# FFN down stage: M7, two slots of M3, M4, the rest of M3, M2; token chunks 0 and 1 updated, normed and turned within it

## What is computed

```
def rmsnorm(x, w):
    y = xf * lax.rsqrt(jnp.mean(xf * xf, axis=-1, keepdims=True) + RMS_EPS)
    return (y * w.astype(jnp.float32)).astype(x.dtype)

def swiglu(h, w_gate, w_up, w_down):
    return (jax.nn.silu(h @ w_gate) * (h @ w_up)) @ w_down

Layer i:  x += 1/2 * post(SwiGLU_1(pre(x)))
          x += post(Mixer_i(pre(x)))   Mixer_even = [GLA heads | Mamba-2 SSD heads], Mixer_odd = MLA
          x += 1/2 * post(SwiGLU_2(pre(x)))
```

## Time and profile before

| | |
|---|---|
| median of 3 runs | 2123.82 us (2123.49 to 2124.54) |
| profiled execution | 2123.88 us |
| its span | 2121.9 us |
| TensorE busy | 2086.2 us, 98% |
| VectorE busy | 1257.0 us, 59% |
| ScalarE busy | 865.7 us, 41% |
| mean granted TensorE clock | 0.993 |
| HBM traffic | 174 GB/s over the span |

### The profile page before, as it was taken

The page is one execution under the profiler, slowest core; times in us unless marked ns, Lnnn a source line. Parts: engine busy times, 40 slices in busy tenths (PEclk is TensorE's granted clock), DMA queues, the critical chain, the costliest instruction groups (busy, mean ns, idle before and its releaser), DMA issues.

```text
span 2121.9 us, 26132 instructions
## 1 busy us (share of the span) xinstructions
PE 2086.2 (98%) x10362; PEld 1750.5 (82%) x10362; DVE 1257.0 (59%) x1819; ACT 865.7 (41%) x1255; POOL 88.7 (4%) x79
## 2 busy tenths in 40 slices
PE   9999999999999999999999999999999999999998
PEld 8888877888888888988887788888787779888877
DVE  6444567476666644645457755445775646445576
ACT  5222355444545543422235532224545444222354
POOL 0000001000000000000000100000014100000000
PEclk9999999999999999999999999999999999999999
DMA  7566684232111213565677375757733124666694
GB/s 267 204 232 211 216 310 154 85 93 60 60 60 60 70 55 134 199 237 199 226 251 264 126 259 191 238 204 259 254 104 125 55 70 143 215 220 226 199 319 142
DMA packets 144412, 371.28 MB, mean 175 GB/s; under 512 B 10354, under 2 KB 10994, under 8 KB 144291
## 3 DMA queue, kind: packets, MB, share of 16 engines
q1 hardware_dynamic: 83440, 229.14, 34.0%
q10 hardware_dynamic: 60850, 140.47, 17.4%
HBM read 297.22 MB, written 71.30 MB: 174 GB/s over the span
## 4 chain that ended last, share of the span: by engine, by line
PE 92%; DVE 4%; issue 2%; ACT 1%; POOL 1%; DMA 0%; ACTq 0%; POOLq 0%; DVEq 0%
PE ps L1137 18%; PE ps L1139 18%; PE ps L1138 18%; PE ps L1145 9%; PE ps L1147 9%; PE ps L1146 9%; PE ps L1452 1%; DVE w_lo L1786 1%; PE ps L1671 1%; PE ps L1700 1%; PE ps L1164 1%; PE ps L1520 1%; DVE normed L1792 1%; PE ps L1675 1%; PE ps L1376 1%
## 5 line engine op out<-in xcount | busy, mean ns | idle before, releaser
L1137 PE MATMUL ps<-h_hi,w_hi 128*128 128x512 f32 (+1 forms) x1832 | 683.3, 373 | 12.9 <-DVE h_lo L1786 12.6
L1139 PE MATMUL ps<-h_hi,w_lo 128*128 128x512 f32 (+1 forms) x1832 | 677.2, 370 | 0.0
L1138 PE MATMUL ps<-h_lo,w_hi 128*128 128x512 f32 (+1 forms) x1832 | 677.1, 370 | 0.0
L577 ACT ACTIVATE w_hi<-raw 128x1024 fp32r<-128x1024 f32 x432 | 454.2, 1057 | 527.3 <-PE ps L1139 338.6
L1786 DVE TENSOR_TENSOR w_lo<-raw,w_hi 128x1024 fp32r<-128x1024 f32 x417 | 502.6, 1221 | 152.2 <-ACT w_hi L577 151.1
L1137 PEld LDWEIGHTS ps<-h_hi,w_hi 128*128 128x128 f32 x1832 | 348.4, 190 | 72.2 <-DVE h_lo L1786 13.9
L1139 PEld LDWEIGHTS ps<-h_hi,w_lo 128*128 128x128 f32 x1832 | 348.3, 190 | 57.7
L1138 PEld LDWEIGHTS ps<-h_lo,w_hi 128*128 128x128 f32 x1832 | 348.6, 190 | 55.9 <-issue 0.2
L1786 DVE TENSOR_TENSOR extra<-a_rows,ps 128x512 f32<-128x512 f32 x88 | 60.5, 688 | 404.0 <-PE ps L1139 380.9
L1145 PE MATMUL ps<-w_hi,a_split 128*128 128x512 f32 x616 | 241.6, 392 | 9.3 <-DVE update L1786 9.3
L1146 PE MATMUL ps<-w_lo,a_split 128*128 128x512 f32 x616 | 240.6, 391 | 0.0
(11 more groups left out here) (237 smaller groups left out, 2233.9 us busy)
## 6 DMA issues: line engine op xcount, KB each, us to landing
raw<-in_w_gate_up SPq DMA_DIRECT2D x176, 512.0 KB, 4.6
a_rows<-in_w_down ACTq DMA_DIRECT2D x44, 1024.0 KB, 9.7
sums<-a_rows ACTq DMA_DIRECT2D x44, 1024.0 KB, 7.8
raw<-sums SPq DMA_DIRECT2D x80, 512.0 KB, 5.2
raw<-in_w_down SPq DMA_DIRECT2D x60, 512.0 KB, 5.3
spilled<-extra ACTq DMA_DIRECT2D x44, 512.0 KB, 4.8
normed<-spilled ACTq DMA_DIRECT2D x44, 512.0 KB, 5.9
raw<-in_w_vg SPq DMA_DIRECT2D x16, 512.0 KB, 3.5
```

Source lines behind the costliest of these rows:

```text
L577: return nc.scalar.activation(to, source, ACT.Copy, scale=scale)
L1137: nc.tensor.matmul(to, w_h, hi, start=first, stop=False)
L1138: nc.tensor.matmul(to, w_h, lo, start=False, stop=False)
L1139: return nc.tensor.matmul(to, w_l, hi, start=False, stop=last)
```

## The change

The order becomes M7 (six slots), M3 (two), M4 (six), M3 (four), M2 (six). Refinements and reloads get new places. Chunks 0 and 1 go through squares, update, norm and turn inside the stage. The sums c21 and c11 are written to rows of their own (`late_sum`, in `extra`) instead of over `update`, and `scale_late` writes their scaled form to `update`. The diff, cut:

```diff
-    for m in range(GROUPS - 2):
-        order += [("M7", m), ("M3", m)]
-    order += [(name, m) for name in ("M7", "M3") for m in (GROUPS - 2, GROUPS - 1)]
-    return order + [("M4", m) for m in range(GROUPS)] + [("M2", m) for m in range(GROUPS)]
+    order += [("M7", m) for m in range(GROUPS)] + [("M3", m) for m in range(2)] + [("M4", m) for m in range(GROUPS)]
+    return order + [("M3", m) for m in range(2, GROUPS)] + [("M2", m) for m in range(GROUPS)]
...
-REFINED_AFTER = [min(2 * j + 4, 23) for j in range(PAIRS)]
+REFINED_AFTER = [3 + (9 * j + 2) // 5 for j in range(PAIRS)]
 JOB_PAIRS = (6, 2)
-RELOAD_AFTER = [min(2 * j, 19) for j in range(PAIRS)]
+RELOAD_AFTER = [max(0, REFINED_AFTER[j] - 5) for j in range(PAIRS)]
...
+        late_sum = [extra[:, (2 + c) % 4, :] for c in range(NC)]
...
+                if b - 1 in FFN_OF:
+                    root_f(b, 0)
+                    root_f(b, 1)
+                    if b < N_SUB:
+                        root_x(b, 0)
+                        root_x(b, 1)
+                for c in range(2 if b - 1 in FFN_OF else 0, NC):
...
                     act.wait_ge(c21_done if c < 2 else c11_done, 2 * FFN_OF[b - 1] + c % 2 + 1)
-                    mean_square(chunk(update, c, 0), stat(SSF1, b, c))
+                    mean_square(late_sum[c], stat(SSF1, b, c))
...
+                if b - 1 in FFN_OF:
+                    square0(b, 2)
+                    square0(b, 3)
+                    if b < N_SUB:
+                        split_high(first)
+                        high_of_h(b, 0)
+                        split_high(first + 1)
+                        high_of_h(b, 1)
+                    square1(b, 2)
+                    if b < N_SUB:
+                        split_high(first + 2)
+                        square_x(b, 2)
+                        split_high(first + 3)
+                    square1(b, 3)
+                    if b < N_SUB:
+                        if b == ODD:
+                            odd_inputs()
+                        high_of_h(b, 2)
+                        square_x(b, 3)
+                        high_of_h(b, 3)
+                        if b not in (EVEN, ODD):
+                            split_high(first + 4)
+                            split_high(first + 5)
+                    return
...
+                for k in range(C12_AFTER + 1):
...
+                    if k == C22_AFTER + 1:
                         square0(s + 1, 0)
                         square0(s + 1, 1)
-                    if k == C12_AFTER + 2:
-                        square0(s + 1, 2)
-                        square0(s + 1, 3)
+                    if k == C21_AFTER:
+                        square1(s + 1, 0)
+                        square1(s + 1, 1)
+                    if k == C21_AFTER + 1 and s + 1 < N_SUB:
+                        square_x(s + 1, 0)
+                        square_x(s + 1, 1)
...
                     last.then_inc(slot_done, 1)
+                    if name == "M2" and s + 1 < N_SUB:
+                        turn_chunk(s + 1, m)
...
                             last = down_product(f, at + k, name, part, 2 * m + part, c)
                         if c:
                             last.then_inc(slot_done, 1)
-                            if k == tail + TAIL // 2 - 1 and s + 1 < N_SUB:
-                                turn_chunk(s + 1, 1)
                     if c == 0:
                         last.then_inc(chunk_done, 1)
-                        if s + 1 < N_SUB:
-                            turn_chunk(s + 1, 0)
...
+                    dve.wait_ge(square_done, squares_before(b, "E", c))
                     stt(chunk(update, c, 1), chunk(update, c, 1), -0.5, four(gain_post[:, T:D]), ALU.mult, ALU.mult).then_inc(update0_done, 1)
...
+            def scale_late(b, c):
+
+                dve.wait_ge(c21_done if c < 2 else c11_done, 2 * FFN_OF[b - 1] + c % 2 + 1)
+                dve.wait_ge(gain_post_in, 16 * b)
+                stt(chunk(update, c, 0), four(late_sum[c]), 0.5, four(gain_post[:, 0:T]), ALU.mult, ALU.mult).then_inc(update1_done, 1)
+
+            def mean_f(b, c):
+
+                dve.wait_ge(square_done, squares_before(b, "F", c))
+                if c >= 2:
+                    dve.wait_ge(square_done, squares_before(b, "E", c))
+                ts(stat(MEANF, b, c), stat(SSF0, b, c), stat(SSF1, b, c), EPS, ALU.add, ALU.add).then_inc(meanf_ready, 1)
...
-                tt(chunk(update, c, 0), chunk(update, c, 0), four(ps[:, 4 + c, :]), ALU.add).then_inc(c11_done, 1)
+                tt(four(late_sum[c]), chunk(update, c, 0), four(ps[:, 4 + c, :]), ALU.add).then_inc(c11_done, 1)
...
+                if b - 1 in FFN_OF:
+                    update0(b, 2)
+                    update0(b, 3)
...
+                    split_low(first)
+                    low_of_h(b, 0)
+                    split_low(first + 1)
+                    low_of_h(b, 1)
+                    add_c11(b, 2)
+                    scale_late(b, 2)
+                    mean_f(b, 2)
+                    add_update(b, 2)
+                    split_low(first + 2)
+                    mean_x(b, 2)
+                    add_c11(b, 3)
+                    scale_late(b, 3)
+                    norm_x(b, 2)
+                    mean_f(b, 3)
+                    split_low(first + 3)
+                    add_update(b, 3)
+                    low_of_h(b, 2)
+                    mean_x(b, 3)
+                    norm_x(b, 3)
+                    low_of_h(b, 3)
+                    if b not in (EVEN, ODD):
+                        split_low(first + 4)
+                        split_low(first + 5)
+                    return
...
+                for k in range(C12_AFTER + 1):
...
-                            add_bank(chunk(update, c, 0), chunk(update, c, 0), "M4", c, c21_done)
+                            add_bank(four(late_sum[c]), chunk(update, c, 0), "M4", c, c21_done)
...
+                    if k in (C22_AFTER + 2, C22_AFTER + 3):
+                        update0(s + 1, k - C22_AFTER - 2)
+                    if k == C21_AFTER:
+                        scale_late(s + 1, 0)
+                        scale_late(s + 1, 1)
+                        mean_f(s + 1, 0)
+                        mean_f(s + 1, 1)
+                        add_update(s + 1, 0)
+                    if k == C21_AFTER + 1:
+                        add_update(s + 1, 1)
+                    if k == C21_AFTER + 2 and s + 1 < N_SUB:
+                        mean_x(s + 1, 0)
+                        mean_x(s + 1, 1)
+                        norm_x(s + 1, 0)
+                    if k == C21_AFTER + 3 and s + 1 < N_SUB:
+                        norm_x(s + 1, 1)
```

85 lines of the change are left out of this document (28 added, 57 removed).

## The result

| | before | changed kernel |
|---|---|---|
| median | 2124.18 us (4 runs) | 2113.09 us (4 runs, 2111.91 to 2117.45) |
| ratio | | 0.995, 95% interval 0.9938 to 0.9962 |

The change makes the kernel 0.5% faster, 11.1 us, where 8.5 were forecast. The profiled execution of it took 2117.45 us, 4.4 above its median. A second profile of the same kernel took 2112.91 (span 2111.1); places and waits are read from that one, and the first is quoted where the two differ.

What follows compares the result with a forecast made beforehand. TensorE, busy 2086.2 of 2121.9 us, was taken as the bound. Boundary gains of 10.25 us less 0.65 in the last stage gave -9.6, the clock +1.1, sum -8.5: 2115.4 us from 2123.88, range 2109.0 to 2121.5.

Steps and rivals of the forecast that it cites:

- the last stage: Last down stage, nothing to turn: +1.15 us at M7's last slot, -0.5 at v, 0.65 lost; chain behind last matmul stays.
- the clock term: Behind turn 0's wait, one clock fall of 1.7 us in each of two boundaries, partly given back: +1.1 us.
- part 4: Late sums in own rows: scaling takes 0.60 us beside the square instead of waiting for it; already in the walk.
- Part 1: Product order in down stages: the 0.50 us wait for v goes in three, -1.5 us; u2 wait stays, M4 costs 0.
- Part 2: Refinements: M7's last slot waits about 1.15 us for pair 10 in each of four down stages, +4.6 us.
- Part 3: Chunks 0 and 1 early: waits of 2.0 us at turn 0, 1.4 at turn 2, 0.2 at turn 3; h_lo's 4.19 goes.
- Cancelled: Rival: VectorE further behind through 2.06 us roots, clock falls at turns 0 and 2 of all boundaries; 2122.7 us, chance 0.15.
- The value of the lone root: POOL root with no split behind it: 0.55 us, taken for roots moved into the down stage instead of 2.06.
- Paces used: Durations taken for the walk: two-pair down slot 2.72 us, 512-column VectorE operation 0.60, POOL root 0.55 to 0.93, once 2.06.
- The rule of the Trainium skill: GpSimd meets SBUF contention from two-input VectorE instructions: moved roots near 2.06 us, some 1.1 us worse per boundary.
- Clean: Rival: clock stays up in all down stages, weight's high half not late, turn 0 waits 0.5 us; 2109.6 us, chance 0.12.
- Refinements too late: Rival: refinements two slots late for M7, which waits 1.15 + 5.44 us in each of four stages; 2137 us, chance 0.07.

Runs made afterwards that it cites:

- no cover: All of M3 run ahead of M4 and both turns put back at their old places, against the changed kernel: 2124.72 us, ratio 1.0004 to the kernel before.

## Why the prediction was right, point by point

**The verdict and the size.** 2115.4 was forecast, 2113.1 measured; the mechanism is the one forecast. That the number is so near is luck in part, for several terms were off. Between the two profiles whose spans are compared above, the boundaries are 2.1 us better than forecast, the last stage 0.5 and the clock term 1.1, together 3.7; the falls behind u2, 0.7 worse in this pair, and the opening, 0.7, give back 1.4. That is -8.5 - 3.7 + 1.4 = -10.8, the difference of the spans. The largest error is one that the total doesn't show (part 4).

**Part 1.** The wait for v is gone (it was 0.50, 0.49 and 0.48 in three stages; in the third, at half clock, there was none); u2 stays at 1.95. M4 waits for nothing. Right. The sum, though, takes the 0.5 in all four stages, in each boundary and in the last stage, where part 1 names three.

**Part 2.** 1.15 was forecast at M7's last slot, 0.98 measured, in four stages. The mechanism is shown from both sides: one slot earlier takes it away, one later adds 2.71.

**Part 3, turn 0.** 2.0 was forecast, 1.57 and twice 1.58 measured. Counted from M4's end at 341.1 in the first profile, x of chunk 0 starts after 5.6 us (5.7 forecast), ScalarE's late weight after 10.1 (10.3), and the first half of `normed` ends after 13.9 (14.0). The walk of the queues held within 0.2 us. What it had wrong was the other side: TensorE comes to the turn after 12.4 and not 12.2, and starts when the first half of `normed` is there, where the 2.0 was counted to the second. Turn 2 was forecast at 1.4 in the same way (its first half at 32.6 against 31.6 gives 1.0) and measured 1.12, 0.91 and 0.88. The 0.2 at turn 3 is not there. The 4.19 for `h_lo` went as forecast.

**The clock.** The step that failed is "one fall in each of two boundaries": behind turn 0 the clock did not fall once, in this kernel or in any other of the study. The analogy with the 1.94 us waits for u2, "one in four", did not carry over to a wait of 1.57, and the term of +1.1 is 0.

**The last stage.** +0.65 was forecast, +0.18 measured. Up to the last matmul it is +0.54 (61.00 against 60.46 us from the mark; 0.98 less 0.48). The chain behind it was said to stay. It shortened by 0.36, from 6.99 to 6.63. From the add to the mean it is 1.48 us in both; the gain is the root's, 0.55 instead of 0.93. Before, the scaling (two SBUF inputs, 2116.90, 0.68 us) ran beside the root; now it runs beside the square, and VectorE does nothing beside the root. POOL's last root, before and in the second profile after:

```profile
2117.07 0.93 POOL L542 TENSOR_TENSOR stats<-stats,minus_half 128x1 f32<-128x1 f32 x1 [3.83 <-DVE stats L1789]
```

```profile
2106.67 0.55 POOL L546 TENSOR_TENSOR stats<-stats,minus_half 128x1 f32<-128x1 f32 x1 [4.21 <-DVE stats L1816]
```

That is part 4 again.

**Part 4, the own rows, was mis-attributed.** The step reads "already in the walk above", with no price. The walk did use it, so the total is not hurt, but a reader learns the wrong thing from it. With the sums in place, and the scaling still ahead of the mean, the gain shrinks from 0.54% to 0.11%, because 0.9 us of standing still on VectorE at two places push turn 2 from 0.9 or 1.1 us to 2.4, and the clock then falls each time. How much of that is the rows and how much the place of the scaling was not measured. I had rated a similar delay only in *Cancelled*, and by another cause, slow roots.

**What it is worth, part by part.** The order, the early turns and the own rows are not separable. Of 0.54%, 0.22% is left without the early turns, 0.11% without the rows, and nothing without cover and early turns. Each lost piece shows up as the same thing, a turn 2 that waits 2.4 to 3.8 us and costs the clock. All three relieve VectorE on the way to `normed` of chunk 2, at different places. From M7's mark VectorE reaches chunk 2's sum after 61.9 us in the changed kernel, 63.1 with late turns and 64.0 without cover as well; from there to `normed` it is 6.5 us with rows of their own and 7.8 with the sums in place.

**The roots and the rule.** Where VectorE stood still for them, two roots took 1.06 us together, 0.53 each; with a split behind, one took 1.46 (POOL's timeline, first profile):

```profile
353.72 1.06 POOL L550 TENSOR_TENSOR stats<-stats,minus_half 128x1 f32<-128x1 f32 x2 [6.56 <-DVE stats L1816]
...
374.40 1.46 POOL L546 TENSOR_TENSOR stats<-stats,minus_half 128x1 f32<-128x1 f32 x1 [2.22 <-DVE stats L1816]
```

The value of the lone root was the right one to take for these. The trace of the kernel before has 1.46 twice as well, for the roots of x of chunks 0 and 1 (354.64 and 360.15, with a split behind), which *Paces used* leaves out. The rule of the Trainium skill (GPSIMD Engine Reference, Key points) agrees with the 1.46, but the roots moved into the down stage fall where VectorE waits for them, and so meet no contention.

**The rivals.** *Clean* is nearer to the truth than its 0.12 says: the clock stayed up at the turns and 2113.1 lies between it (2109.6) and the forecast. But turn 0 did wait 1.57, so it is not that case. *Refinements too late* is what the kernel with pair 10 behind slot 22 shows. One slot gave 2133, where the rival's own sum has 2126 for one and 2137 for two: it left out the falls of the clock. *Cancelled* is what the kernel with sums in place shows, 2123.0 for 2122.7, by another cause; that the numbers agree is chance.

## What to carry to other kernels

Norming a tile early pays only if the in-order queue that delivers it also keeps up for the next tile: after each edit look at the next place where TensorE waits, since there half of a saved wait came back (2.4 of 4.7 us here), and once all of it (0.55 us at turn 2, given back at turn 3). A wait is worth more than its length where it is long enough to bring the clock down: within a down stage and at its boundary bring the long ones under 1.8 us first, where no fall was seen, even by turning one long wait into two short ones (1.95 into 0.21 and 1.59, with u2 first in the kernel before). In a hand-written order, the place of a producer relative to the waits ahead of it (a split that waits for ScalarE) is worth a sweep of one or two slots both ways; here one slot was worth 4 us on one side and 21 on the other.

## What the runs showed of the hardware

The granted clock after a wait of TensorE, over the thirteen profiles of this study, in the down stages and at their boundaries:

| the wait | lower level (1.2 of 2.4 GHz) at its end or right behind |
|---|---|
| 0.21 to 0.43 (u2) | 0 of 16 |
| 0.98 (pair 10) | 0 of 28 |
| 0.88 to 1.76 (turn 2) | 0 of 24 |
| 1.57 and 1.58 (turn 0) | 0 of 18 |
| 1.59 to 1.64 (v) | 0 of 4 |
| 1.94 and 1.95 (u2) | 12 of 33 |
| 2.43 and 2.46 (turn 2, sums in place) | 3 of 3 |
| 3.57 to 3.79 (turn 2, pair 10) | 9 of 10 |
| 4.2 (`h_lo`, both kernels with the old order) | 6 of 6 |

A fall lasted 3.4 us, sometimes 6.8, and some began within the long wait itself; half of what TensorE works through of it is lost, 1.6 us behind u2 in the changed kernel. It is not the length alone: of the few u2 waits that were longer by chance, 3.21 brought a fall and 3.13 and 2.92 did not. And the 1.8 us hold only for where they were seen. Near 8 us of the span, among the small matmuls of the start, five of the thirteen profiles have a wait of 0.74 to 1.31 us for `normed`, and all five have a fall there. What decides between these, and within the 33 at 1.94, was not found.

A root on POOL took 0.53 to 0.55 us where VectorE waited for it, 0.93 beside a scaling of 0.68 us, 1.46 beside a split of 1.2, and 2.06 beside a scaling and a split, in all cases VectorE operations with two SBUF inputs.

Loads of `raw` landed late now and then, in the last slots ahead of M7. In one of the two profiles of the changed kernel ScalarE waited 2.09 us for one, with the DMA engines busy 0.98 of the time around it (1128 to 1132 us), and the wait for u2 became 3.21. The same stands behind the 2.92 (slot 22) and the 3.13 (no cover), there in the last down stage. It is three of thirteen profiles, 1.0 to 1.3 us each time and perhaps the clock, so a profile alone can differ from another of the same kernel by that much.
